# Router weights and index tables: another place in SBUF, and the router's loads after the merge

## The reference

```python
x = x + merged @ w_out
h = rms_norm(x, norm2_w)                      # 544 x 1024
g_logits = h @ w_gr + b_gr                    # 4 groups
e_logits = h @ w_er + b_er                    # 32 experts
# top-1 group, then the top 2 of its 8 experts, with weights from both softmaxes
out[token] += weight * (silu(h @ w_g[e]) * (h @ w_u[e])) @ w_d[e]
```

## Time and profile before

| | us |
|---|---|
| median of 3 runs | 1543.01 |
| lowest, highest | 1538.64, 1545.41 |
| the profiled execution, its time | 1545.41 |
| the profiled execution, its span | 1543.7 |

### The profile page before, as it was taken

How to read it: one execution, slowest core, us unless ns; L and a number is a source line. 1 busy time by engine, 2 the same in 40 slices (tenths; PEclk the granted TensorE clock), 3 DMA queues, 4 the chain that set the end, 5 groups by cost and what they waited for, 6 DMA issues and landing times.

```text
span 1543.7 us, 22239 instructions
## 1 busy us (share of the span) xinstructions
PE 1353.7 (88%) x8780; PEld 804.6 (52%) x8780; DVE 395.2 (26%) x721; ACT 353.5 (23%) x566; POOL 87.9 (6%) x146
## 2 busy tenths in 40 slices
PE   6999988996999999987699999979988887788873
PEld 5847534464666767655488886544333333333321
DVE  2013243324434343543111102341110111011103
ACT  2023224222545444564200001120100000000000
POOL 3000000002000000200000000010110011001000
PEclk9999999897999998999799999988998999899987
DMA  6114200003899998999893115029999999999995
GB/s 222 55 55 131 82 0 0 0 0 109 303 353 349 352 347 319 374 386 385 279 338 129 55 55 221 28 104 394 419 425 427 426 427 425 425 426 426 425 393 189
DMA packets 119641, 395.94 MB, mean 256 GB/s; under 512 B 17076, under 2 KB 25285, under 8 KB 107251
## 3 DMA queue, kind: packets, MB, share of 16 engines
q1 hardware_dynamic: 109506, 380.41, 63.6%
q0 software_dynamic: 5984, 11.18, 2.1%
q10 hardware_dynamic: 4048, 2.93, 0.6%
HBM read 386.06 MB, written 16.27 MB: 261 GB/s over the span
## 4 chain that ended last, share of the span: by engine, by line
PE 73%; DVE 6%; issue 6%; DMA 6%; SPq 5%; ACT 3%; ACTq 0%; POOLq 0%; DVEq 0%
PE ps L1116 16%; PE ps L941 8%; PE ps L1139 7%; PE ps L638 7%; PE ps L764 5%; PE ps L641 4%; DMA arena<-in_cache_k 4%; PE ps L944 4%; PE ps L1003 4%; PE ps L775 3%; SPq L362 2%; PE ps L797 2%; SPq L354 2%; PE ps L693 2%; PE ps L697 1%
## 5 line engine op out<-in xcount | busy, mean ns | idle before, releaser
L1116 PE MATMUL ps<-arena 128*64 128x512 f32 x512 | 256.1, 659 | 65.8 <-issue 64.5
L1117 PE MATMUL ps<-arena 128*64 128x512 f32 x512 | 256.6, 660 | 0.0
L1116 PEld LDWEIGHTS ps<-arena 128*64 128x64 f32 x512 | 74.7, 152 | 213.5 <-issue 211.1
L764 PE MATMUL ps<-ident,arena 128*128 128x128 f32 x1024 | 148.8, 291 | 27.1 <-DMA arena<-in_cache_k 21.9
L764 PEld LDWEIGHTS ps<-ident,arena 128*128 128x128 f32 x1024 | 117.4, 147 | 97.6 <-issue 66.2
L1342 ACT ACTIVATE arena<-ps 128x512 f32<-128x512 f32 x192 | 108.5, 595 | 172.1 <-PE ps L764 171.9
L941 PE MATMUL ps<-mixers,arena 128*128 128x272 f32 x512 | 121.7, 399 | 7.6 <-DMA arena<-in_w_in 7.6
L638 PE MATMUL ps<-mixers,arena 128*128 128x272 f32 x512 | 121.2, 399 | 0.5 <-DVE mixers L1489 0.5
L941 PEld LDWEIGHTS ps<-mixers,arena 128*128 128x128 f32 x512 | 98.9, 194 | 28.9 <-DMA arena<-in_w_in 8.0
L638 PEld LDWEIGHTS ps<-mixers,arena 128*128 128x128 f32 x512 | 98.4, 193 | 21.5 <-DVE mixers L1489 0.6
L641 PE MATMUL ps<-arena,mixers 128*128 128x512 f32 (+1 forms) x240 | 105.4, 594 | 0.0
(11 more groups left out here) (327 smaller groups left out, 1377.4 us busy)
## 6 DMA issues: line engine op xcount, KB each, us to landing
arena<-in_cache_k SPq DMA_DIRECT2D x256, 256.0 KB, 5.2
arena<-in_cache_v SPq DMA_DIRECT2D x256, 256.0 KB, 5.2
arena<-in_w_gate_exp SPq DMA_DIRECT2D x32, 2048.0 KB, 32.0
arena<-in_w_up_exp SPq DMA_DIRECT2D x32, 2048.0 KB, 36.6
arena<-in_w_down_exp SPq DMA_DIRECT2D x22, 2048.0 KB, 37.2
mixers<-in_w_down_exp SPq DMA_DIRECT2D x10, 2048.0 KB, 37.4
arena<-in_w_in SPq DMA_DIRECT2D x7, 2048.0 KB, 9.4
arena<-in_w_in SPq DMA_DIRECT2D x8, 1024.0 KB, 14.3
```

Of the source, the lines that this page charges most:

```text
L764: last = turn(ps[:, TURN + j % 2, P * c:P * c + P], kring[n % 3][:, j, P * c:P * c + P], ident[:, :])
L1116: mm(ps[0:BLK, 1 + u, :], own, wgv[w][:, k, :], start=k == 0, stop=k == KD - 1)
L1117: last = mm(ps[BLK:P, 1 + u, :], own, wuv[w][:, k, :], start=k == 0, stop=k == KD - 1)
```

## The change

The router's weights get no tile of their own: `wr` lies in the last part of `mixers`, where the outputs of the recurrent mixer were, which the branch products have read by then; `w2c` and `r_b` lie in `route`. As `route` and that part of `mixers` are in use until the merge, the five loads are issued behind the wait for `merged`, and behind `route_zero`, which VectorE raises once it has cleared them. VectorE clears `wr` and fills the unused group columns of `r_b`, which GpSimd did at the start. The index lists get small tiles of their own, and two of the five tables `in_pos` change places.

```diff
+        wr = mixers[:, 8192:8192 + KD * 40].rearrange("p (a b) -> p a b", a=KD)
         in_pos = [carve(o, 2, P) for o in (18432, 18688, 18944)] + [
-            each(v, 2) for v in (arena[:, 40960:40960 + 2 * P], attn_masks[:, 2 * P:4 * P])]
-        router_w = sb("router_w", [P, KD * 40 + KD + 40])
-        wr = router_w[:, 0:KD * 40].rearrange("p (a b) -> p a b", a=KD)
-        w2c, r_b = router_w[:, KD * 40:KD * 40 + KD], router_w[:, KD * 40 + KD:]
+            each(v, 2) for v in (attn_masks[:, 2 * P:4 * P], sb("in_pos", [P, 2 * P])[:, :])]
...
+        load_i = sb("load_i", [P, NPAIR], I32)
+        store_i = sb("store_i", [P, NE], I32)
+        extra_lists = sb("extra_lists", [P, 2 * NOVF], I32)
...
+        w2c, r_b = small(KD), small(40)
...
-        load_i, store_i, extra_lists = (small(k).bitcast(I32) for k in (NPAIR, NE, 2 * NOVF))
...
@@ GpSimd, at the start
-                         (new_neg, 0.0), (in_b, 1.0), (router_w, 0.0)):
+                         (new_neg, 0.0), (in_b, 1.0)):
...
-            chain(nc.gpsimd.memset(r_b[:, NG:8], -BIG))
@@ ScalarE, ahead of the attention
             act.wait_ge(S("heads_normed"), 2 * CT)
-            act.wait_ge(S("constants"), 2)
-            load(w2c, a["norm2_w"][0].rearrange("(p k) -> p k", k=KD), "router_inputs")
-            load(wr[:, :, 0:NG], a["w_group_router"][0].rearrange("(p k) n -> p k n", k=KD), "router_inputs")
-            load(wr[:, :, 8:8 + NE], a["w_expert_router"][0].rearrange("(p k) n -> p k n", k=KD), "router_inputs")
-            load(r_b[:, 0:NG], a["b_group_router"].to_broadcast([P, NG]), "router_inputs")
-            load(r_b[:, 8:8 + NE], a["b_expert_router"].to_broadcast([P, NE]), "router_inputs")
             load(lbr[:, :, :], a["lb_logits"].rearrange("(o r) c -> o r c", o=1).to_broadcast([P, 2, W]), "lb_loaded")
@@ ScalarE, behind the sigmoids
             act.wait_ge(S("merged"), KD)
+            act.wait_ge(S("route_zero"), 1)
+            load(w2c, a["norm2_w"][0].rearrange("(p k) -> p k", k=KD), "router_inputs")
+            load(wr[:, :, 0:NG], a["w_group_router"][0].rearrange("(p k) n -> p k n", k=KD), "router_inputs")
+            load(wr[:, :, 8:8 + NE], a["w_expert_router"][0].rearrange("(p k) n -> p k n", k=KD), "router_inputs")
+            load(r_b[:, 0:NG], a["b_group_router"].to_broadcast([P, NG]), "router_inputs")
+            load(r_b[:, 8:8 + NE], a["b_expert_router"].to_broadcast([P, NE]), "router_inputs")
             nc.scalar.preload_act_table_set("natural_log_exp_and_others")
@@ VectorE, behind the merge
             chain(v.memset(route, 0.0))
+            chain(v.memset(flat(wr), 0.0))
             chain.wait()
             chain(v.memset(r_low, -BIG))
-            v.memset(r_gs, 1.0).then_inc(S("route_zero"), 1)
+            chain(v.memset(r_gs, 1.0))
+            v.memset(r_b[:, NG:8], -BIG).then_inc(S("route_zero"), 1)
```

## The result

| | before | changed |
|---|---|---|
| median of 7 runs each, us | 1542.97 | 1549.37 |
| lowest to highest, us | 1538.64 to 1545.41 | 1545.84 to 1558.99 |
| profiled execution: time, span, us | 1545.41, 1543.7 | 1551.85, 1550.1 |

The ratio is 1.0064, 95% interval 1.0041 to 1.0088: slower by 6.3 to 13.6 us, 9.9 us in the middle. The medians of the table alone differ by 6.4 us; the runs of each kernel scatter by nearly 7 us and more. The seven of the changed kernel are among 24 executions on record, whose median is 1552.0 us. The forecast was 1555.5 us, +12.5 us.

What follows compares the result with a forecast made beforehand. PE was taken to set the pace until about 1020 us, then the expert weights; 9.5 us of wait plus 3.0 us of clock gave +12.5 us, a median of 1555.5 us, with 1546 to 1562 us for 8 in 10.

Steps and rivals of the forecast that it cites:

- The joint of the two stages: PE delays between 950 and 1027 us delay the restart of the expert weight stream and the end by the same amount.
- Layout, GpSimd, ScalarE at 136 us, VectorE's fills: New buffer places, dropped start fills, issues gone at 136 us, added fills at 950 us: each taken as 0.
- The wait of TensorE: Before the first router product, PE waits for the fifth load, landing at 969.4 us: 9.5 us, between 7.5 and 11.7.
- One packet for one beside the stream: At 954 to 964 us, queues alternate single packets, so about 280 load packets pass beside expert 1's weights.
- The drain itself: After the weight stream ends at about 965.0 us, the remaining 2230 load packets need 2.4 us on empty engines.
- now all is issued already: Reason for taking 2.4 us to drain: all five loads would be issued before the stream ends, issuing taking 2.9 us.
- the tail of 1.0 us and the completion of 1.0 us: Two terms added after the drain for the fifth load's landing: 1.0 us tail (0 to 2.3) and 1 us completion.
- slower still: Rival: beside the stream issues back up, loads run their whole 7.75 us after 965.0 us; 15.8 us, 1558.8 us, chance 0.15.
- Several small runs per turn: Rival: engines take many small runs between stream packets, loads land at 960 to 966 us; 5.7 us, 1548.7 us, chance 0.13.
- The clock: After its wait before the first router product, PE runs at half clock for some 5 us: 3.0 us, 2.5 to 3.6.
- The sum: All terms for the whole kernel: 0 + 0 + 9.5 + 3.0 = 12.5 us slower, between 10.0 and 15.3.
- Faster: Rival: removing the issues at 136 us starts attention up to 2.9 us earlier, late loads hidden; 1540.1 us, chance 0.03.

Runs made afterwards that it cites:

- late_only: Kernel before with its old layout, only the five router loads moved behind the merge and route_zero; ratio to before 1.0073.
- head3: Kernel before with the five router loads moved from 136 us to attention head 3, where nothing waits for them; ratio to before 1.0008.
- wide_runs: Changed kernel with both router matrices loaded as one run per partition into a staging area, 640 runs instead of 2432; ratio to before 1.0071.
- kept_busy_9: Changed kernel with 9 extra, unread products on TensorE ahead of the first router product; ratio to before 1.0062.
- a_again: The changed kernel, unedited, traced a second time; ratio to before 1.0069.
- b_again: The kernel before, unedited, run once more against itself; ratio 1.0015.
- down_waits: Changed kernel, third matrix of expert 1 (2 MB of 6) issued only after the five router loads landed; ratio to before 1.0076, timed again 1.0044.

## Why the prediction was right, point by point

*The joint of the two stages* was right: 12.5 us between merge and restart came out of the change, and the stage behind ran at 426 GB/s as before. From the restart to the end of the span it is 515.9 us before and 516.4 us changed, and the other traces scatter between 513.1 and 516.3 whatever the delay, so nothing was given back that shows.

*Layout, GpSimd, ScalarE at 136 us, VectorE's fills: 0.* Right within what can be told. late_only gives the whole loss without the new layout; head3 finds no gain (1.0008). The 0.33 us fill was estimated at 0.27. One part of this was wrong: ScalarE's five issues were to take 2.9 us "as before" and its first row scale to start 8 us after the merge. They took 14.3 us, and the row scale started 19.5 us after the merge.

*The wait of TensorE: 9.5 us* (7.5 to 11.7). Measured 9.39 and 9.14, but the parts of it were not all as summed. One packet for one beside the stream was right. The DMA view of the changed kernel, 954 to 955 us, 957 to 958 us and 958 to 959 us:

```profile
q1 hardware_dynamic: 28, 0.43, 99.5%
q10 hardware_dynamic: 28, 0.00, 1.6%
...
q1 hardware_dynamic: 25, 0.20, 46.9%
q10 hardware_dynamic: 695, 0.02, 41.1%
...
q10 hardware_dynamic: 1062, 0.11, 88.3%
```

28 and 28, and then, as the stream ends, 695 and 1062 in one us each. The drain itself went about as summed: from 957 to 960 us 1985 packets of the scalar queue passed, where 2230 in 2.4 us had been taken. The term that failed is the premise behind it, "now all is issued already". The fourth issue was held up until 959.5 us, the fifth load went out at 959.56 us only, when the stream was all but over, and it landed 3.3 us later, at 962.9 us. The sum had reached nearly the same landing (21.0 us after the merge, measured 21.1) by a drain, a tail and a completion behind the stream: 3.3 us from the landing of the stream's last matrix to that of the fifth load, measured 3.0. That these agree is partly luck. No run shows the tail of 1.0 us and the completion of 1.0 us by themselves. The part of the "slower still" rival in which issues back up did happen, though the loads did not need their whole 7.75 us afterwards. Without the block, but with all 2432 runs, the landing was not measured; wide_runs, with neither, had it 18.9 us after the merge.

*"Several small runs per turn"* failed by the same rows. The rule of the Trainium skill (page "DMA: Bandwidth & Descriptors", section "Queues, rings and completion order"), by which an engine drains some 9 to 17 descriptors of a row before it switches, would have brought the loads in during the stream, as the prediction read it. That holds only if the stream gives up its turn after each of its 16 KB runs. If it too drains 9 to 17 of them, the two queues get on one for one again, in bursts. The trace shows no bursts either: from 953 to 957 us it counts 27 and 26, 28 and 28, 27 and 27, 25 and 25 packets in one us each, over 16 engines, where each run is one packet. So single runs took turns, and here the measurement decides.

*The clock: 3.0 us* (2.5 to 3.6). 3.04 in the first trace and 1.59 in the second, 1.5 to 3.0 over all kernels that idled. The mechanism is shown by kept_busy_9; the lower bound was too high. It was read from 5 us at half speed in one place of one trace, and in a_again half speed lasted only some 3.4 us. In the row of kept_busy_9, 1.43 us of idle cost no clock.

*The sum: 12.5 us.* Merge to restart it is 12.5 and 10.8 us in the two traces, 9.9 and 10.6 us by the timed ratios. That the first trace met 9.5 + 3.0 so closely is luck in the clock term. The median of seven, 1549.37 us, is inside the range for 8 in 10 (1546 to 1562 us) but below the forecast's own (1553 to 1559 us). It is nearer to the 1548.7 us of "several per turn" than to 1555.5 us, and its 6.4 us above before are less than the 7.7 us that the prediction asked of a median. So these seven times alone could not have told the forecast from that rival; the traces and the ratio do. The median of all 24 is 1552.0 us, and the second series differed by 10.8 us (1550.94 against 1540.16).

*The signs.* The prediction called itself wrong if the fifth load landed before 963 us. It landed at 962.9 us, but in an execution that reached the merge 6.6 us earlier; counted from the merge it was 0.1 us later than forecast. A sign given as a clock time has to be read against such a mark.

*"Faster"* seemed to be there in the first trace, with its head start of 6.6 us, twice what that rival could give; b_again and head3 showed that this was scatter.

## What to carry to other kernels

A load that is moved "to where its buffer is free" also moves to where other transfers are: look at the DMA share there, at the end of the stream that runs there, and at the count of the load's runs. 166 KB in 2432 runs waited for a 6 MB stream of weights that were first used some 86 us after they had landed (966.1 and 1052.65 us in the trace of before). Holding back a third of that stream gave back 5.0 us of idle, a quarter of the runs 1.85 us, and one wait on SP, putting the urgent load first, all of it. When an engine idles ahead of dense work, add the fall of TensorE's clock to the price. And before a shift in one trace is explained, trace the unedited kernel again.

## What the runs showed of the hardware that was not expected

A queue full of small runs beside a stream holds up the engine that issues. ScalarE's third and fourth load took 4.43 and 8.38 us to issue beside the stream (4.20 and 8.35 in a_again, 3.86 and 3.93 in down_waits with its shorter stream, 4.55 and 3.46 in its second run), 0.69 and 0.67 with the stream held back, and 0.46 and 0.47 when the loads had 640 runs. ScalarE's table load and first row scale behind them started at 960.0 and 961.3 us. That cost nothing here: wide_runs, where the row scale started at 952.0 us, has the same 79.37 us beside its idle and its clock. How many runs the queue takes before it holds up an issue was not measured.

Reads of one DRAM row for all partitions may be dear out of proportion to their 18 KB: with the biases first, 4 us passed with 0.84 instead of 0.97 of the engines' time in use and 30% less bandwidth. This is one trace, and its next 4 us do not show it.

The unedited kernel reaches the same point of its program up to 4.3 us apart in two executions (944.1 and 948.4 us), while the stretch behind it repeats to 0.03 us.
